# Four pieces of TensorE work stand one projection unit earlier in the gated delta mixer

## The reference

```python
def gated_deltanet_mixer(h, w_in, conv_w, a_log, dt_bias, o_norm, w_out):
    proj = h @ w_in
    qkv = jax.nn.silu(causal_dwconv(proj[..., :GDN_QKV_W], conv_w))
    q, k, v = _split(qkv, (GDN_QK_W, GDN_QK_W, GDN_V_W))
    gate, b_raw, a_raw = _split(proj[..., GDN_QKV_W:], (GDN_V_W, GDN_HEADS, GDN_HEADS))
    q = l2norm(q.reshape(B, S, GDN_HEADS, GDN_DK))
    k = l2norm(k.reshape(B, S, GDN_HEADS, GDN_DK))
    beta = jax.nn.sigmoid(b_raw)
    g = -jnp.exp(a_log) * jax.nn.softplus(a_raw + dt_bias)
    o = gated_delta_chunked(q, k, v.reshape(B, S, GDN_HEADS, GDN_DV), g, beta)
    o = gated_rmsnorm(o, gate.reshape(B, S, GDN_HEADS, GDN_DV), o_norm)
    return o.reshape(B, S, GDN_V_W) @ w_out
```

## Time and profile before

| | us |
|---|---|
| median of 3 runs | 1882.49 |
| lowest and highest run | 1880.45, 1883.49 |
| the profiled execution, its own time | 1880.45 |
| its span in the profile | 1878.7 |

### The profile page before, as it was taken

The page is one execution under the profiler, slowest core; times in us unless marked ns, Lnnn a source line. Parts: engine busy times, 40 slices in busy tenths (PEclk is TensorE's granted clock), DMA queues, the critical chain, the costliest instruction groups (busy, mean ns, idle before and its releaser), DMA issues.

```text
span 1878.7 us, 25589 instructions
## 1 busy us (share of the span) xinstructions
PE 1768.4 (94%) x10362; PEld 1111.9 (59%) x10362; DVE 773.8 (41%) x1545; ACT 309.1 (16%) x665; POOL 52.1 (3%) x89
## 2 busy tenths in 40 slices
PE   4999999999999989998999999999999799999998
PEld 3886744444444338888856544444443587768875
DVE  5657422222222136778853222222211557535173
ACT  0111310100000012431231101000000232220121
POOL 0100000000000000000000000000000010100000
PEclk9999999999999989999889999999999899999999
DMA  9977599999999985764566999999999674215301
GB/s 404 348 273 297 202 371 425 426 425 425 425 425 426 426 340 211 271 254 178 200 271 242 395 424 425 425 424 425 424 425 422 264 268 173 90 45 202 118 23 45
DMA packets 82115, 576.86 MB, mean 307 GB/s; under 512 B 9148, under 2 KB 11452, under 8 KB 12800
## 3 DMA queue, kind: packets, MB, share of 16 engines
q1 hardware_dynamic: 70992, 494.65, 64.2%
q0 software_dynamic: 10992, 80.43, 11.4%
HBM read 573.98 MB, written 1.06 MB: 306 GB/s over the span
## 4 chain that ended last, share of the span: by engine, by line
PE 67%; DMA 20%; SPq 7%; DVE 4%; issue 2%; ACT 1%; DVEq 0%; ACTq 0%
PE ps L335 65%; DMA wbuf<-in_moe_gu 8%; SPq L1403 6%; DMA hma<-in_moe_gu 5%; DMA slab<-in_moe_gu 4%; PE ps L339 2%; DVE hma L551 1%; DMA wP<-in_moe_gu 1%; SPq L1418 1%; DMA slab<-in_ada 0%; SPq L1413 0%; DVE slab L2958 0%; DVE slab L2955 0%; ACT slab L342 0%; DMA wbuf<-in_od_out 0%
## 5 line engine op out<-in xcount | busy, mean ns | idle before, releaser
L335 PE MATMUL ps<-slab 128*128 128x128 f32 (+9 forms) x3224 | 549.7, 360 | 13.1 <-DMA slab<-in_moe_gu 9.7
L335 PEld LDWEIGHTS ps<-slab 128*128 128x128 f32 (+4 forms) x3224 | 345.8, 172 | 193.9 <-issue 166.1
L335 PE MATMUL ps<-hma,wbuf 128*128 128x256 f32 (+1 forms) x1520 | 342.5, 386 | 0.9 <-DVE hma L347 0.9
L335 PE MATMUL ps<-wbuf,slab 128*32 128x512 f32 (+3 forms) x1088 | 317.2, 617 | 18.6 <-DMA wbuf<-in_moe_gu 18.5
L335 PEld LDWEIGHTS ps<-hma,wbuf 128*128 128x128 f32 (+1 forms) x1520 | 289.4, 192 | 49.1 <-issue 8.2
L342 ACT ACTIVATE slab<-ps 128x256 f32<-128x256 f32 (+4 forms) x125 | 58.4, 476 | 952.6 <-PE ps L335 932.8
L335 PE MATMUL ps<-hma,slab 128*32 128x512 f32 (+2 forms) x472 | 186.3, 610 | 10.0 <-DMA hma<-in_moe_gu 10.0
L335 PEld LDWEIGHTS ps<-wbuf,slab 128*32 128x32 f32 (+2 forms) x1088 | 97.6, 135 | 159.6 <-issue 122.3
L1621 DVE TENSOR_TENSOR slab<-ps,slab 128x256 f32<-128x256 f32 x44 | 18.7, 425 | 393.7 <-ACT slab L342 393.7
L335 PE MATMUL ps<-slab,cst 128*32 128x512 f32 (+5 forms) x490 | 130.1, 551 | 5.3 <-ACT slab L342 5.3
L551 DVE SCALAR_TENSOR_TENSOR hma<-wbuf,cs,hma 128x1024 f32<-128x1024 f32 x102 | 130.8, 1282 | 8.0 <-DMA wbuf<-in_ada 4.7
(11 more groups left out here) (274 smaller groups left out, 1492.0 us busy)
## 6 DMA issues: line engine op xcount, KB each, us to landing
wbuf<-in_moe_gu SPq DMA_DIRECT2D x89, 1024.0 KB, 24.4
slab<-in_moe_gu SPq DMA_DIRECT2D x71, 1024.0 KB, 19.8
wbuf<-in_ada POOLq DMA_DIRECT2D x60, 1024.0 KB, 6.3
wbuf<-in_moe_d SPq DMA_DIRECT2D x55, 1024.0 KB, 25.7
hma<-in_moe_gu SPq DMA_DIRECT2D x47, 1024.0 KB, 24.0
cst<-in_moe_gu SPq DMA_DIRECT2D x34, 1024.0 KB, 23.2
wbuf<-in_od_in SPq DMA_DIRECT2D x30, 1024.0 KB, 4.8
hma<-in_moe_d SPq DMA_DIRECT2D x25, 1024.0 KB, 25.3
```

The costliest lines, as they stand in the source:

```text
L335: return e.matmul(o, lhsT, rhs, start=start, stop=stop, skip_group_check=skip)
```

## The change

Only the order of the lines in `delta_pe` changes. No engine gets or loses an instruction, and the orders of DVE, ACT, POOL and SP stay as they were. Five things stand elsewhere: the head sums of the queries go ahead of unit 6, those of the keys ahead of unit 10, the turning of the keys ahead of unit 13, `products(1)` ahead of unit 15 (with unit 14 now behind `products(0)` and the turning of the values), and `rows_pe` goes from the middle of level 0 to the place ahead of it.

```diff
-            for n in range(3, 7):
+            for n in range(3, 6):
                 unit_pe(n)
             heads_pe(e, "d_q", 8, S(4, 8, 256))
+            unit_pe(6)
             ada_sum_pe(e, 8)
             unit_pe(7)
             unit_pe(8)
             ada_turn_pe(e, 8)
             unit_pe(9)
+            heads_pe(e, "d_k", 8, S(4, 8, 256))
             unit_pe(10)
-            heads_pe(e, "d_k", 8, S(4, 8, 256))
             ada_sum_pe(e, 9)
             unit_pe(11)
             ada_turn_pe(e, 9)
             unit_pe(12)
-            unit_pe(13)
             turn("d_kt", d_k, "d_ktc", lambda i: ("d_kn", i))
             ada_sum_pe(e, 10)
-            unit_pe(14)
+            unit_pe(13)
             ada_turn_pe(e, 10)
             turn("d_vt", d_v, "d_vtc", lambda i: ("d_cv", 8 + i))
             products(0)
+            unit_pe(14)
+            products(1)
             unit_pe(15)
-            products(1)
             for i in range(4):
                 decays(i)
+            rows_pe(e, "r1", mods[:, 8, :])
...
                     t.then_inc(*P.up("d_x", lv, i))
-                if lv == 0:
-                    rows_pe(e, "r1", mods[:, 8, :])
```

## The result

| | before, us | after, us |
|---|---|---|
| median | 1882.49 | 1892.75 |
| lowest and highest run | 1880.45, 1883.49 | 1889.12, 1894.63 |
| the profiled execution, its own time | 1880.45 | 1894.76 |
| its span in the profile | 1878.7 | 1893.0 |

The changed kernel takes 1.0053 times as long, interval 1.0039 to 1.0068 (five runs of each). That is +10.3 us, where +5.9 was forecast. The direction and the place were right, the size was not, and 1892.75 lies above the range of 1884.3 to 1891.3. Later the same kernel was timed again beside 23 runs of the kernel before: 1.0049, interval 1.0032 to 1.0066, so +9.2 us. The profiled executions are 14.3 apart, and that is too much to explain by the change: about 3 us of it are there ahead of the first moved line, and about 2 behind the whole stage.

A forecast was written before the change was run, and what follows sets the result against it. PE was taken to bound this mixer's projections. New waits of 8.3 us, less 2.45 won, plus 0.1, gave +5.9 us; added to the median of 1882.49, the forecast was 1888.4 us, range 1884.3 to 1891.3.

The forecast's parts named there:

- Head sums of the queries: Ahead of unit 6: PE waits 2.0 us for the first square, which ACT's order puts behind the copy of unit 5.
- Head sums of the keys and unit 10 in bank 3: PE waits 2.0 us for ACT's squares ahead of unit 10, then 1.6 us for DVE's read of the bank.
- Turning of the keys and unit 13: PE waits 2.0 us for DVE's scaled keys, 0.4 for its pace, then 0.3 for bank 4 ahead of unit 13.
- Rival A: The clock falls in PE's new gaps, once or twice, making the change +7.6 to +9.3 us; chance 0.15.
- What is won: At level 0, PE's 2.45 us wait for DVE's masked copy goes; later DVE work gives back 0.1 us.
- what is late next: Behind the first masked copy in level 0: DVE's second masked copy, with three subtractions behind it, costs +0.1 us.
- Products(1), unit 15, rows_pe: Ahead of the levels: these swap places on a busy PE with inputs long ready, counted as 0.
- The trap behind it: ACT's unit 15 copy and table load delay the decays; without rows_pe as cover this path adds about 1 us.
- The queues: SP's output-weight and router-row loads come up to 10 us later and POOL's follow DVE; counted as 0.
- B: As a rival: part of the shift is absorbed behind the mixer by load waits, +1 to +3 us; chance 0.13.
- C: Moved pieces find inputs ready and the wait at 854.94 goes, so the kernel is faster, -2.5 us; chance 0.05.
- D: The new PE waits exist but are smaller, +2 to +3.7 us; chance 0.09.

The follow-up runs named there:

- e8: The kernel before with only the head sums of the queries moved ahead of unit 6; 1886.41 us against 1887.92, ratio 1.0007.
- e9: The kernel before with the query head sums moved and, in ACT's order, SiLU of unit 3 and squares ahead of the copy of unit 5; 1884.51 us, ratio 0.9989.
- e3: The kernel before with only the turning of the keys moved ahead of unit 13, units 13 and 14 behind it; 1889.21 us, ratio 1.0026.
- e4: The kernel before with only products(1) moved ahead of unit 15 and rows_pe ahead of level 0; 1883.82 us, ratio 0.9992.
- e6: The kernel before with products(1) and rows_pe moved, and SP's first expert-stage loads issued behind the last level; 1883.37 us, ratio 0.9994.
- e10: The kernel before with only products(1) moved ahead of unit 15, rows_pe left in level 0; 1883.26 us against 1887.92, ratio 0.9979.
- e7: The kernel before with only SP's first expert-stage loads issued later, behind level 0, so they fall into the levels; 1885.54 us, ratio 0.9997.
- e5: The changed kernel with SP's first expert-stage loads issued later, behind the last level; 1891.78 us, ratio to the kernel before 1.0039.
- e2: The kernel before with only the two groups of head sums moved, queries ahead of unit 6, keys ahead of unit 10; 1891.99 us, ratio 1.0039.
- e11: The kernel before, unchanged, in a second profile; one run, 1885.55 us.
- e12: The kernel before with products(1) moved ahead of unit 15 and eight extra small PE products far ahead; one run, 1889.19 us.
- e1: The changed kernel run once more as it is; 1895.16 us against 1883.71 for the kernel before, ratio 1.0049.

## Why the prediction missed, step by step

**Head sums of the queries, 2.0.** Right. The turn of task 8 moved from 782.88 to 788.12, 5.24; less the 3.19 of unit 3 (740.32 - 737.13) that is 2.05. e8 shows it alone (A 2.0) and e9 that ACT's order is the cause (0.0).

**Head sums of the keys and unit 10 in bank 3, 2.0 + 1.6.** Right. The turn of task 9 moved by 816.92 - 808.02 = 8.90, so by 3.66 more. Both gaps have the forecast releasers.

**Turning of the keys and unit 13, 2.0 + 0.4 + 0.3.** The wait was right, the sum too small. The sum of task 10 stood at 823.89, and has one unit (6.93) less ahead of it: 829.20 + 6.93 - 823.89 = 12.24, less 8.90 is 3.34. The eight records at 829.20 take 0.44 more, so 3.8 instead of 2.7. Of this 1.1 us too much, the clock is the cause: transposes and sum took 3.25 + 1.08 us here and 2.44 + 0.64 in e3, where it did not fall, 1.25 more. That is Rival A, at one of four gaps, with a price of about 1.1 instead of the 1.7 worked out; that part of the slow stretch was hidden by the pace of DVE is an inference. The wait of 0.3 for bank 4 vanished in it.

**What is won, -2.45 + 0.1.** This is the step that failed. It took the end of DVE's wait as the end of waiting. The wait did go, and up to the product behind it the sum holds with the terms as measured: 2.05 + 3.66 + 3.8 - 2.45 = 7.1, against A of 6.8; I can't place the 0.3. What I wrote as "what is late next" named only DVE's second masked copy. PE's own supply of instructions was late next, and took 0.49 + 1.95 = 2.44 us, while a wait of 0.65 us for a masked copy of level 1 went. e4, e6 and e10 show this without any other part of the change: A is -3.0, -3.0 and -2.9, B only -1.1, -0.8 and -0.7. That the wait of 2.45 us had covered the supply before is not shown. It did cover one packet, which started at 853.33, 0.84 us into the wait. But the packet behind the stop of 1.95 us is the next one. It was in time before, with no wait but one of 0.65 us between the product a packet ahead and the one that needs it, and late in e7 with the wait of 2.44 us in place.

**Products(1), unit 15, rows_pe, 0.** Right up to the level stage. The trap behind it was smaller than worked out: without `rows_pe` as a cover (e10) A is -2.9, with it (e4) -3.0, so some 0.2 us (2.87 and 3.04) and not 1.

**The queues, 0.** SP's load of the router row went from 843.12 to 857.99, 15 us later and not up to 10. e5 shows what that was worth: up to 0.7 us, the first `issue` stretch. The step looked at who needs the loads and not at what they pass on the way.

**The sum.** Forecast 5.9, measured 9.0 in the profile (B). Up to the product behind the masked copy A is 6.8, 0.9 more than forecast; the clock is the one cause that I can name. Behind it come another 2.3. Of these 2.44 - 0.65 = 1.8 are the two idle stretches, and 0.5 stands at the same two places, where the products start later than the idle time alone makes them. The times give +9.2 to +10.3, with an interval of 6.0 to 12.8 over both measurements. They agree with 9.0, but would not exclude 6.8: the late supply is shown by the profiles, not by the times.

**The rivals.** B fell: the load of the expert stage moved with PE. C fell at its first gap, and D with the sizes. A was right once in the whole: the clock fell at one of the four gaps, and there was no cold start behind each of them. In e2, e3, e7 and e8 the clock fell at the wait of 2.45 us that stays there; in before, e9 and e11 it did not fall at the same wait. So whether one such gap costs the clock is not fixed by its length.

**What stays open.** Why a packet of instructions comes late in the changed kernel. It was too late in eight profiles and in time in six. Two causes remain: loads in flight, which e7 shows to be enough in one profile, but of which POOL's loads of the modulation weights were never held back; and a PE that runs closer behind its supply once its wait is gone. The second is argued and not shown by a run of its own, and e7, where the stop came with the wait in place, speaks against it as the only one. Open too is why e10 is 4 us faster in its times and 0.7 in its profile.

## What to carry to other kernels

Taking away a wait of PE doesn't show that nothing else is late behind it. In a long run of small products, count such a wait as won only after looking for `issue` stretches behind it, and for loads in flight when the next packet of instructions is due. Before a piece is moved ahead, look at the order of the engine that feeds it: here one gap of four, and by the same pattern a second, came from one copy ahead of the squares in ACT's order. And with banks in rotation, each moved piece changes whose reader the next one waits for.

## What the runs showed of the hardware

- PE's instructions arrive in packets of 16,384 bytes on q8, one each 3.6 to 6 us in the levels of after (from 866.93 on). When one was late, PE stood still until 2.3 to 2.7 us behind its start, behind the same count of products in all eight profiles, whatever the work there was.
- That packet started 0.3 to 1.1 us behind the product 127 records ahead of the one that needs it where the DMA engines were nearly idle (six profiles), and 2.9 to 4.3 us behind it where they were at 0.8 to 1.0 (eight profiles).
- In e12 eight products of 8 columns, 2.7 us in all, were followed by a unit of 9.37 us instead of 7.17, with the granted clock at 0.50, its level of 1.2 GHz, in this window (columns as in the earlier trace rows):

```profile
730.00:735.00 5.00, 4.94 (x16) 4.20 (x16) 3.05 (x7) 0.41 (x3) 0.50 (x1) 0.50 0.21 88
```

- The clock fell behind the gap of 1.82 us ahead of the transposes in after, e1 and e5, but not in e3, where the gap was 1.94 us, and not behind the gaps of 1.81 us ahead of the head sums, in any profile. At the wait of 2.45 us at level 0 it fell in e2, e3, e7 and e8, and not in before, e9 and e11.
